# Modulation of a diffusion layer: seven of twelve weight blocks multiplied in high and low parts, two row tiles scaled by ScalarE

## Chip, cores and metric

One core of a Trainium2 chip. The metric is the device time of one execution in microseconds, median of several runs. The two last decimals are the hardware profiler's.

## What is computed

The reference is one layer of a token generator: adaLN-modulated RMSNorm, two token mixers, a merge, a mixture of experts. The change lies in its first step, the modulation of both streams (1024 latent tokens modulated by `c`, 256 context tokens by `c_ctx`), D = 1024:

```python
mod = silu(c) @ w_mod + b_mod           # 6 * 1024 columns
shift, scale = mod[..., :1024], mod[..., 1024:2048]
h = rms_norm(x, g) * (1 + scale) + shift
...
```

The further four thousand columns of `mod` are gates and the shift and scale of the second norm. All in float32; the big products of the kernel use the type fp32r, with each operand split into a high part (the value rounded to fp32r) and a low part (the rest).

## The kernel before

The program is a row of stages with a barrier between them; the first after the constants is `front` (line 173), the next `project_qk`. Each stage is written by hand as five instruction streams with semaphores: SyncE (the weights' DMA queue), ScalarE, GpSimd, TensorE, VectorE.

`front` works on twelve blocks of 512 columns of `w_mod` (`NB = 12`), 128 partitions x 8 x 512 in float32, 2 MB each, in three slots of `fr_w`. SyncE loads a block when the one three before is multiplied (L217), its bias behind it (L223). TensorE multiplies (`rows`, L312): the stationary side is `fr_c`, two columns (silu of `c` and of `c_ctx`), the moving side 512 columns of the weights, eight pieces k that add up in `fr_rows_ps`, float32, which the engine works off as sixteen records. VectorE takes the 2 x 512 result and adds the bias (`take`, L352). TensorE then turns it into columns for the first four blocks (`out`, L323, four transposes into 128 x 8), or spreads it over 128 partitions for the other eight (L326), ScalarE moves it out of PSUM (`move`, L271 and L277), and SyncE stores the spread rows (L230).

Blocks 4 to 8 carry two of the ten token tiles each (128 tokens, `tiles_before`): ScalarE normalises a tile (`normalise`: square with sum L255, L257, L260, scale L264) and asks for the next but one (L250); TensorE turns it (L334); VectorE scales and shifts it in eight pieces (`leave`, L361) and casts the high part (L366), GpSimd subtracts the low part (L302). Tiles 0 and 1 are normalised before the first `move`. At the start of the stage GpSimd makes the masks of later stages (`build_masks`, L147 to L170), among them 28 affine selects on `level_mask` (L162, L164), each waiting for the one before.

The streams around the change:

```python
            normalise(0)
            normalise(1)
            for n in range(NB):
                move(n)
                for t in tiles_before(n):
                    if t + 2 < NT:
                        normalise(t + 2)
```

```python
            for n in range(NB):      # TensorE
                rows(n)
                for t in tiles_before(n):
                    turn(t)
                out(n)
```

## Time and profile before

| | |
|---|---|
| median of 3 runs | 2454.72 us (2452.33 to 2458.88) |
| profiled execution | 2456.33 us, span 2454.6 us |
| mean granted clock of TensorE | 0.942 |
| TensorE busy | 2175.8 us, 89% of the span |
| VectorE, ScalarE, GpSimd busy | 1420.3, 1013.2, 854.0 us |
| `front`, first transfer to the first of the next stage | 6.1 to 131.7 us |

Busy shares are means over stages with different limits; the stage in question is 125 of 2454 us, 5%. A row of the order of time gives when an instruction started, how long it lasted, and in brackets how long its engine had been idle and who ended that; a row of the waits gives the sum for one waiting line. L numbers are lines of the kernel before, and lines of the changed kernel where the text says so.

### The profile page before, as it was taken

How to read it: one execution, taken by the hardware profiler on the slowest of the kernel's cores; microseconds unless marked ns; L12 is line 12 of the kernel's file. 1: busy time of each engine (PE TensorE's matmuls, PEld its weight loads, DVE VectorE, ACT ScalarE, POOL GpSimd, SP SyncE). 2: the span in 40 equal slices, each digit the busy share in tenths (PEclk: the TensorE clock that was granted, in tenths of full speed). 3: DMA queues.
4: the chain of work that ended last, by engine and by line, in shares of the span. 5: the costliest groups of instructions: out<-in, count | busy, mean ns of one | idle time of the engine just before them, and what ended most of it. 6: DMA issues, size and time to landing. Idle time of an engine off the chain costs nothing. (4 is left out here: it accounts for less than half of the span.)

```text
span 2454.6 us, 26795 instructions
## 1 busy us (share of the span) xinstructions
PE 2175.8 (89%) x10286; PEld 1757.6 (72%) x10286; DVE 1420.3 (58%) x1711; ACT 1013.2 (41%) x1266; POOL 854.0 (35%) x630
## 2 busy tenths in 40 slices
PE   6979997998798994899999779999659999999992
PEld 1268886887687883788888657788557788887882
DVE  0529642110333323888988445434258899998993
ACT  1422310111244443455555344432226666766762
POOL 5300000110356662567766422210113344443541
PEclk9989998999899996899999989999859999999996
DMA  7733226211754665243454386563359966369425
GB/s 277 252 72 101 74 56 219 82 48 47 248 172 156 184 154 184 86 129 109 128 134 121 86 263 190 174 194 117 109 214 338 366 221 198 98 196 341 146 53 163
DMA packets 263146, 398.75 MB, mean 162 GB/s; under 512 B 27302, under 2 KB 187174, under 8 KB 256236
## 3 DMA queue, kind: packets, MB, share of 16 engines
q1 hardware_dynamic: 233324, 243.90, 31.3%
q0 software_dynamic: 27968, 147.89, 19.2%
q10 hardware_dynamic: 1728, 5.25, 0.6%
q8 instruction: 83, 1.36, 0.2%
q14 instruction: 43, 0.35, 0.0%
HBM read 401.68 MB, written 88.67 MB: 200 GB/s over the span
## 5 line engine op out<-in xcount | busy, mean ns | idle before, releaser
L2600 DVE TENSOR_TENSOR ex_w_lo<-ex_raw,ex_w_hi 128x2048 fp32r<-128x2048 f32 x186 | 415.9, 2285 | 38.5 <-ACT ex_w_hi L2462 38.2
L2462 ACT ACTIVATE ex_w_hi<-ex_raw 128x2048 fp32r<-128x2048 f32 x182 | 337.8, 1909 | 170.9 <-DMA ex_raw<-in_w_up_dram,rt_w_rows 88.9
L816 POOL DMA_DIRECT2D vals<-rows_stage x40 | 21.8, 545 | 449.7 <-ACT rows_stage L808 449.7
L2332 POOL DMA_INDIRECT ex_raw<-in_w_up_dram,rt_w_rows x60 | 78.0, 1299 | 137.3 <-DVE ex_w_lo L2600 126.1
L2025 DVE TENSOR_TENSOR mo_w_lo<-mo_w,mo_w_hi 128x1024 fp32r<-128x1024 f32 x48 | 59.2, 1234 | 98.6 <-ACT mo_w_hi L1922 98.6
L1557 PEld LDWEIGHTS gl_lv_ps<-gl_q_level,gl_k_level 128*128 128x128 f32 x896 | 108.2, 194 | 11.2 <-issue 8.3
L2332 POOL DMA_INDIRECT ex_raw<-in_w_down_dram,rt_w_rows x30 | 51.9, 1730 | 183.2 <-DVE ex_w_lo L2600 176.9
L1557 PE MATMUL gl_lv_ps<-gl_q_level,gl_k_level 128*128 128x64 f32 x896 | 110.4, 276 | 3.7 <-DVE gl_scores L1687 2.0
L808 ACT ACTIVATE rows_stage<-rows_ps 128x512 f32<-128x512 f32 x40 | 23.9, 598 | 214.2 <-PE rows_ps L785 214.2
L901 PE MATMUL gl_u_ps<-half_hi,gl_u_w_hi 128*128 128x512 f32 x256 | 107.8, 421 | 4.4 <-ACT gl_u_exp L919 4.4
L901 PE MATMUL ml_u_ps<-half_hi,ml_u_w_hi 128*128 128x512 f32 x256 | 104.9, 410 | 6.5 <-ACT ml_u_exp L919 6.5
L2391 PE MATMUL ex_g_ps<-ex_w_hi,ex_x_hi 128*128 128x512 f32 x248 | 102.4, 413 | 6.5 <-DVE ex_x_lo L2605 6.5
L2391 PE MATMUL ex_y_ps<-ex_w_hi,ex_hidden_hi 128*128 128x512 f32 x248 | 100.3, 404 | 7.1 <-DVE ex_w_lo L2600 7.1
L2136 PE MATMUL mo_ps<-mo_branch_hi,mo_w_hi 128*128 128x512 f32 x256 | 104.8, 409 | 1.4 <-POOL mo_branch_lo L1990 1.0
L2137 PE MATMUL mo_ps<-mo_branch_hi,mo_w_lo 128*128 128x512 f32 x256 | 102.7, 401 | 0.0
L2138 PE MATMUL mo_ps<-mo_branch_lo,mo_w_hi 128*128 128x512 f32 x256 | 102.6, 401 | 0.0
L903 PE MATMUL gl_u_ps<-half_hi,gl_u_w_lo 128*128 128x512 f32 x256 | 101.3, 396 | 0.0
L902 PE MATMUL gl_u_ps<-half_lo,gl_u_w_hi 128*128 128x512 f32 x256 | 101.2, 395 | 0.0
L903 PE MATMUL ml_u_ps<-half_hi,ml_u_w_lo 128*128 128x512 f32 x256 | 101.1, 395 | 0.0
L902 PE MATMUL ml_u_ps<-half_lo,ml_u_w_hi 128*128 128x512 f32 x256 | 101.0, 395 | 0.0
L2392 PE MATMUL ex_g_ps<-ex_w_lo,ex_x_hi 128*128 128x512 f32 x248 | 99.0, 399 | 0.0
L2393 PE MATMUL ex_g_ps<-ex_w_hi,ex_x_lo 128*128 128x512 f32 x248 | 98.6, 398 | 0.0
(403 smaller groups left out, 6079.3 us busy)
## 6 DMA issues: line engine op xcount, KB each, us to landing
fr_w<-in_w_mod_dram SPq DMA_DIRECT2D x12, 2048.0 KB, 9.8
ml_u_w<-in_w_in_dram SPq DMA_DIRECT2D x32, 512.0 KB, 5.2
gl_u_w<-in_w_in_dram SPq DMA_DIRECT2D x32, 512.0 KB, 5.2
vals<-rows_stage POOLq DMA_DIRECT2D x40, 256.0 KB, 2.3
ml_v<-vals SPq DMA_DIRECT2D x20, 512.0 KB, 4.4
gl_v<-vals SPq DMA_DIRECT2D x20, 512.0 KB, 3.3
qk_w<-in_w_in_dram SPq DMA_DIRECT2D x16, 512.0 KB, 5.0
rows_w<-in_w_in_dram SPq DMA_DIRECT2D x8, 1024.0 KB, 6.5
```

The source lines that it names most:

```text
L901: pe.matmul(self.ps[:, :], a_hi, b_hi, start=(k == 0), stop=False)
L902: pe.matmul(self.ps[:, :], a_hi, b_lo, start=False, stop=False)
L903: last = pe.matmul(self.ps[:, :], a_lo, b_hi, start=False, stop=(k == KD - 1))
L1557: last = pe.matmul(lv_ps[at_l // 2 % 2][:, lv_cols(at_l, h)], kl[:, d, l, h * P:(h + 1) * P], ql[:, l, h * P // 2:(h + 1) * P // 2], start ...
L2136: pe.matmul(out, a_hi, b_hi_, start=(k == 0), stop=False)
L2137: pe.matmul(out, a_lo, b_hi_, start=False, stop=False)
L2138: last = pe.matmul(out, a_hi, b_lo_, start=False, stop=(k == KD - 1))
L2332: pool.indirect_dma_start(out=raw[:, q, :], out_offset=None, in_=sources[q], in_offset=bass.IndirectOffsetOnAxis(ap=w_rows[:, q, b:b + 1], ...
L2391: pe.matmul(dst, a_hi[:, ka], hi[:, q, at:at + 512], start=first, stop=False)
L2392: pe.matmul(dst, a_hi[:, ka], lo[:, q, at:at + 512], start=False, stop=False)
L2462: act.activation(hi[:, q, h], raw[:, q, h], ACT.Copy).then_inc(hi_done[q], 1)
L2600: dve.tensor_tensor(lo[:, q, at], raw[:, q, at], hi[:, q, at].bitcast(F32), ALU.subtract)\
```

## The change

Blocks 0 to 3 and 9 to 11 (`PARTED`) are no longer multiplied in float32. For each of their pieces k ScalarE makes the high part (`weight_hi`), VectorE the low part (`weight_lo`), TensorE multiplies both with a stationary side of four columns: the high parts of `silu(c)` and `silu(c_ctx)`, then their low parts (`c_parts`). High and low pieces lie in rings of three. The result has four rows, which `out` folds to two (`pairs`, `first`). Blocks 4 to 8 are multiplied as before. The last two tiles, 8 and 9, are scaled by ScalarE, out of PSUM, in eight pieces each, and VectorE only casts them. The bias has two slots of four rows, which GpSimd fills with zeros first. Square writes into `fr_xn` instead of a tile of its own, so the wait for the turn stands ahead of it.

```diff
+    PARTED = [n for n in range(NB) if n not in WITH_TOKENS]
+    RING = 3
...
+        LATER = WITH_TOKENS[-1] + 1
+        BY_ACT = (NT - 2, NT - 1)
...
             def normalise(t):
...
+                if t >= 2:
+                    act.wait_ge(turned, t - 1)
+                act.activation(xn[:, j, :], xt[:, j, :], ACT.Square, accum_out=st[:, t, 0:1]).then_inc(stat, 1)
...
+            def weight_hi(n, first, last):
+                act.wait_ge(w_loaded[n % SLOTS], 16 * (n // SLOTS) + 16)
+                for k in range(first, last):
+                    at = piece(n, k)
+                    if at >= RING:
+                        act.wait_ge(piece_done, at - RING + 1)
+                    act.activation(w_hi[:, at % RING, :], wt[:, n % SLOTS, k, :], ACT.Copy).then_inc(w_hi_done, 1)
+
+            def leave(t):
...
+                for k in range(KD):
+                    last = act.activation(ht[:, t % 2, k, :], x_ps[t % 2][:, k * P:(k + 1) * P], ACT.Identity,
+                                          bias=m.mod_col[:, k, stream:stream + 1],
+                                          scale=m.a1[:, k, stream:stream + 1])
+                last.then_inc(scaled_by_act, 1)
...
+            weight_hi(0, 0, KD)
             normalise(0)
-            normalise(1)
             for n in range(NB):
+                if n + 1 in PARTED and n + 1 != LATER:
+                    weight_hi(n + 1, 0, KD)
+                for t in tiles_before(n):
+                    if t in BY_ACT:
+                        leave(t)
                 move(n)
+                if n == 0:
+                    normalise(1)
                 for t in tiles_before(n):
                     if t + 2 < NT:
                         normalise(t + 2)
+                if n + 2 == LATER:
+                    weight_hi(LATER, 0, RING)
+                if n + 1 == LATER:
+                    weight_hi(LATER, RING, KD)
...
+            pool.memset(bias[:, :, :], 0.0).then_inc(bias_cleared, 1)
+            pool.memset(first[:, :], 0.0).then_inc(first_ready, 1)
+            pool.memset(pairs[:, :], 0.0).then_inc(first_ready, 1)
...
+            def rows_in_parts(n):
+                if n >= 2:
+                    pe.wait_ge(row_ready, n - 1)
+                for k in range(KD):
+                    at = piece(n, k)
+                    pe.wait_ge(w_lo_done, at + 1)
+                    out = rows_ps[n % 2][:, :]
+                    pe.matmul(out, c_parts[:, :, k], w_hi[:, at % RING, :], start=(k == 0), stop=False)
...
+            def weight_lo(n, first, last):
+                for k in range(first, last):
+                    at = piece(n, k)
+                    dve.wait_ge(w_hi_done, at + 1)
+                    if at >= RING:
+                        dve.wait_ge(piece_done, at - RING + 1)
+                    dve.tensor_tensor(w_lo[:, at % RING, :], wt[:, n % SLOTS, k, :],
+                                      w_hi[:, at % RING, :].bitcast(F32), ALU.subtract).then_inc(w_lo_done, 1)
...
+            weight_lo(0, 0, KD)
             for n in range(NB):
+                if n + 1 in PARTED and n + 1 != LATER:
+                    weight_lo(n + 1, 0, RING - 1)
                 take(n)
+                if n + 1 in PARTED and n + 1 != LATER:
+                    weight_lo(n + 1, RING - 1, KD)
...
                 for t in tiles_before(n):
                     leave(t)
+                if n + 2 == LATER:
+                    weight_lo(LATER, 0, RING)
+                if n + 1 == LATER:
+                    weight_lo(LATER, RING, KD)
```

The prediction writes hi(n,k) and lo(n,k) for the high and the low part of piece k of block n.

How the change moves instructions, at three places. First ScalarE at the start of the stage, from the tables' loading on, before (L255 to L264 is a normalisation, L250 its next load):

```order
L284 ACT_TABLE_LOAD
L255 ACTIVATE fr_junk,fr_stat<-fr_x 128x1024 [waits fr_x_loaded0]
L257 ACTIVATE fr_stat<-fr_stat,eps 128x1 [waits fr_stat]
L260 ACTIVATE fr_stat<-fr_stat 128x1 [waits fr_stat]
L264 ACTIVATE fr_xn<-fr_x,fr_stat 128x1024 [waits fr_stat]
L250 DMA fr_x<-in_x_dram 128x1024 [waits fr_xn_ready]
L255 ACTIVATE fr_junk,fr_stat<-fr_x 128x1024 [waits fr_x_loaded1]
```

and in the changed kernel (its L303 is a high part, its L286 to L293 a normalisation, its L318 the move to columns):

```order
L303 ACTIVATE fr_w_hi<-fr_w 128x512 [waits fr_w_loaded0]
L303 ACTIVATE fr_w_hi<-fr_w 128x512 x2
L303 ACTIVATE fr_w_hi<-fr_w 128x512 [waits fr_piece_done] x5
L286 ACTIVATE fr_xn,fr_stat<-fr_x 128x1024 [waits fr_x_loaded0]
L288 ACTIVATE fr_stat<-fr_stat,eps 128x1 [waits fr_stat]
L291 ACTIVATE fr_stat<-fr_stat 128x1 [waits fr_stat]
L293 ACTIVATE fr_xn<-fr_x,fr_stat 128x1024 [waits fr_stat]
L279 DMA fr_x<-in_x_dram 128x1024 [waits fr_xn_ready]
L303 ACTIVATE fr_w_hi<-fr_w 128x512 [waits fr_piece_done,fr_w_loaded1]
L303 ACTIVATE fr_w_hi<-fr_w 128x512 [waits fr_piece_done] x7
L318 ACTIVATE mod_col<-fr_out_ps 128x8 [waits fr_out_done]
L286 ACTIVATE fr_xn,fr_stat<-fr_x 128x1024 [waits fr_x_loaded1]
```

Eight high parts stand ahead of normalise(0), eight more behind it, and normalise(1) has moved behind the first move.

Second, VectorE at its start in the changed kernel (L433 is a low part, L442 a take); before, the takes stood here one behind the other:

```order
L433 TENSOR_TENSOR fr_w_lo<-fr_w,fr_w_hi 128x512 [waits fr_w_hi_done] x3
L433 TENSOR_TENSOR fr_w_lo<-fr_w,fr_w_hi 128x512 [waits fr_piece_done,fr_w_hi_done] x7
L442 TENSOR_TENSOR fr_row<-fr_rows_ps,fr_bias 4x512 [waits fr_bias_loaded0,fr_piece_done]
L433 TENSOR_TENSOR fr_w_lo<-fr_w,fr_w_hi 128x512 [waits fr_piece_done,fr_w_hi_done] x8
L442 TENSOR_TENSOR fr_row<-fr_rows_ps,fr_bias 4x512 [waits fr_bias_loaded1,fr_piece_done]
```

Rows that print alike are drawn together: of the seven low parts of the second row five belong to block 0 and two to block 1, so take(0) stands behind lo(1,0) and lo(1,1), and likewise further on.

Third, VectorE around take(8), before (L352 is a take, L361 and L366 scale and cast a tile):

```order
L366 CAST later_hi<-fr_h 128x8x128 [waits fr_scaled]
L361 TENSOR_SCALAR fr_h<-fr_x_ps,a,mod_col 128x128 [waits fr_split_lo,fr_turned]
L361 TENSOR_SCALAR fr_h<-fr_x_ps,a,mod_col 128x128 x7
L366 CAST later_hi<-fr_h 128x8x128 [waits fr_scaled]
L352 TENSOR_TENSOR fr_row<-fr_rows_ps,fr_bias 2x512 [waits fr_out_done,fr_bias_loaded2,fr_rows_done]
L361 TENSOR_SCALAR fr_h<-fr_x_ps,a,mod_col 128x128 [waits fr_split_lo,fr_turned]
```

and in the changed kernel (L451 and L459 are the scaling and the cast):

```order
L451 TENSOR_SCALAR fr_h<-fr_x_ps,a,mod_col 128x128 [waits fr_split_lo,fr_turned]
L451 TENSOR_SCALAR fr_h<-fr_x_ps,a,mod_col 128x128 x7
L459 CAST later_hi<-fr_h 128x8x128 [waits fr_scaled]
L433 TENSOR_TENSOR fr_w_lo<-fr_w,fr_w_hi 128x512 [waits fr_piece_done,fr_w_hi_done] x3
L442 TENSOR_TENSOR fr_row<-fr_rows_ps,fr_bias 2x512 [waits fr_out_done,fr_bias_loaded0,fr_rows_done]
L459 CAST later_hi<-fr_h 128x8x128 [waits fr_scaled_by_act,fr_split_lo,fr_turned] x2
L433 TENSOR_TENSOR fr_w_lo<-fr_w,fr_w_hi 128x512 [waits fr_piece_done,fr_w_hi_done] x7
L442 TENSOR_TENSOR fr_row<-fr_rows_ps,fr_bias 4x512 [waits fr_out_done,fr_bias_loaded1,fr_piece_done]
L433 TENSOR_TENSOR fr_w_lo<-fr_w,fr_w_hi 128x512 [waits fr_piece_done,fr_w_hi_done] x8
```

Three low parts of block 9 stand between the last tile of block 7 and take(8), five behind the casts of tiles 8 and 9, drawn together there with two of block 10.

## Rows read from the trace of the kernel before

**Rows 1.** Waits, 6 to 131 us: who waited for whom; us in total, times, longest.
```profile
DVE fr_row L352 <- PE fr_rows_ps L312: 78.8, 12, 21.5
```

**Rows 2.** Order of time, VectorE: start us, duration us, engine, line, operation, tiles, [idle before].
```profile
26.98 0.68 DVE L352 TENSOR_TENSOR fr_row<-fr_rows_ps,fr_bias 2x512 f32<-2x512 f32 x1 [21.54 <-PE fr_rows_ps L312]
35.12 0.68 DVE L352 TENSOR_TENSOR fr_row<-fr_rows_ps,fr_bias 2x512 f32<-2x512 f32 x1 [7.46 <-PE fr_rows_ps L312]
...
109.06 0.68 DVE L352 TENSOR_TENSOR fr_row<-fr_rows_ps,fr_bias 2x512 f32<-2x512 f32 x1 [2.23 <-PE fr_rows_ps L312]
...
126.76 0.68 DVE L352 TENSOR_TENSOR fr_row<-fr_rows_ps,fr_bias 2x512 f32<-2x512 f32 x1 [8.17 <-PE fr_rows_ps L312]
```

**Rows 3.** Order of time, TensorE's first and last products, its last spread, next stage's first transfer.
```profile
17.97 8.98 PE L312 MATMUL fr_rows_ps<-fr_w,fr_c 128*2 128x512 f32 x16 [12.84 <-DMA fr_w<-in_w_mod_dram]
...
119.69 7.03 PE L312 MATMUL fr_rows_ps<-fr_w,fr_c 128*2 128x512 f32 x16
...
127.49 1.12 PE L326 MATMUL fr_out_ps<-fr_row,fr_first 2*128 2x512 f32 x2 [0.77 <-DVE fr_row L352]
...
131.74 0.39 SPq L449 DMA_DIRECT2D qk_w<-in_w_in_dram  x1
```

**Rows 4.** Order of time, TensorE at 1450 us: fp32r products of 512 columns, back to back.
```profile
1450.64 0.39 PE L2137 MATMUL mo_ps<-mo_branch_hi,mo_w_lo 128*128 128x512 f32 x1
1450.87 0.39 PE L2138 MATMUL mo_ps<-mo_branch_lo,mo_w_hi 128*128 128x512 f32 x1
```

**Rows 5.** Groups by shape (busy us, mean ns of one): a high part, a low part.
```profile
L1929 ACT ACTIVATE mo_branch_hi<-mo_branch 128x512 fp32r<-128x512 f32 x32 | 20.3, 633 | 35.6 <-DVE mo_branch L2020 35.3
...
L2049 DVE TENSOR_TENSOR mo_y_lo<-mo_part,mo_y_hi 128x512 fp32r<-128x512 f32 x16 | 10.9, 684 | 0.0
```

**Rows 6.** Order of time, ScalarE: the first row of normalise(0), and of normalise(1).
```profile
14.81 1.06 ACT L255 ACTIVATE fr_junk<-fr_x 128x1024 bf16<-128x1024 f32 x1 [2.01 <-DMA fr_x<-in_ctx_dram]
...
18.11 1.06 ACT L255 ACTIVATE fr_junk<-fr_x 128x1024 bf16<-128x1024 f32 x1 [0.41 <-ACT fr_xn L264]
```

**Rows 7.** Order of time, GpSimd: selects of the masks, the last at 39.06.
```profile
7.95 1.10 POOL L152 TENSOR_SCALAR_AFFINE_SELECT row_of<-row_of 36x1024 f32<-36x1024 f32 x1
...
12.26 2.12 POOL L162 TENSOR_SCALAR_AFFINE_SELECT level_mask<-level_mask 128x256 int8<-128x256 int8 x1
...
39.06 0.46 POOL L164 TENSOR_SCALAR_AFFINE_SELECT level_mask<-level_mask 128x256 int8<-128x256 int8 x1
```

**Rows 8.** Order of time at 695 us: a GpSimd subtraction, a VectorE addition, both from SBUF.
```profile
695.72 2.42 POOL L890 TENSOR_TENSOR ml_u_w_lo<-ml_u_w,ml_u_w_hi 128x1024 fp32r<-128x1024 f32 x1 [0.20 <-ACT ml_u_w_hi L884]
...
696.80 1.89 DVE L1220 TENSOR_TENSOR ml_expo<-ml_rows,g_col 128x512 f32<-128x512 f32 x1
```

**Rows 9.** The same stretch further on, and all instances of the select (ns min/median/max).
```profile
698.61 0.68 DVE L1222 TENSOR_TENSOR ml_qi<-qm,ml_rows 128x512 f32<-128x512 f32 x1
...
698.84 0.95 POOL L1073 TENSOR_SCALAR_AFFINE_SELECT ml_expo<-ml_expo 128x512 f32<-128x512 f32 x1 [0.70 <-DVE ml_expo L1220]
...
L1073 POOL TENSOR_SCALAR_AFFINE_SELECT ml_expo<-ml_expo x16: 946/949/1088, 638.1 to 900.9; 128x512 f32<-128x512 f32 x16
```

**Rows 10.** Order of time at 1035 us: a one-input multiply on GpSimd, a multiply on VectorE.
```profile
1035.33 1.92 POOL L924 TENSOR_SCALAR gl_u_exp<-gl_u_exp 128x512 f32<-128x512 f32 x1
1036.24 0.72 DVE L1649 TENSOR_TENSOR gl_k_out<-gl_k,gl_exp 128x512 f32<-128x512 f32 x1
```

**Rows 11.** DMA issues of the page: KB each, median us from issue to landing.
```profile
fr_w<-in_w_mod_dram SPq DMA_DIRECT2D x12, 2048.0 KB, 9.8
```

**Rows 12.** Order of time before take(8): GpSimd's lo(7), ScalarE's last of normalise(9).
```profile
97.00 2.35 POOL L302 TENSOR_TENSOR later_lo<-fr_h,later_hi 128x1024 fp32r<-128x1024 f32 x1 [0.93 <-DVE later_hi L366]
97.20 1.15 ACT L264 ACTIVATE fr_xn<-fr_x,fr_stat 128x1024 f32<-128x1024 f32 x1
```

**Rows 13.** Groups by shape: ScalarE out of PSUM.
```profile
L580 ACT ACTIVATE qk_plain<-qk_ps x4: 377/378/379, 276.8 to 366.1; 128x256 f32<-128x256 f32 x4
...
L808 ACT ACTIVATE rows_stage<-rows_ps 128x512 f32<-128x512 f32 x40 | 23.9, 598 | 214.2 <-PE rows_ps L785 214.2
```

**Rows 14.** Windows: us, then busy us of PE, PEld, DVE, ACT, POOL, granted clock, DMA share, GB/s.
```profile
131.00:148.00 17.00, 5.67 (x26) 5.68 (x27) 2.36 (x2) 2.00 (x2) 3.28 (x5) 0.50 0.56 101
```

More of the change, by code:

```diff
@@ L232, in _ @@
                 load(n)
+            sp.wait_ge(bias_cleared, 1)
+            for n in range(2):
                 load_bias(n)
@@ L322, in out @@
                     for q in range(4):
-                        last = pe.transpose(out_ps[j][:, 2 * q:2 * q + 2], row[:, j, q * P:(q + 1) * P],
-                                            m.ident[0:2, 0:2])
-                else:
-                    last = pe.matmul(out_ps[j][:, :], first[:, :], row[:, j, :], start=True, stop=True)
+                        last = pe.matmul(out_ps[j][:, 2 * q:2 * q + 2], row[:, j, q * P:(q + 1) * P], pairs[:, :],
+                                         start=True, stop=True)
+                else:
+                    n_rows = parts_of(n)
+                    last = pe.matmul(out_ps[j][:, :], first[0:n_rows, :], row[0:n_rows, j, :], start=True, stop=True)
                 last.then_inc(out_done, 1)
@@ L337, in _ @@
             pe.wait_ge(c_ready, 1)
[L338 removed]
+            pe.wait_ge(c_split, 2)
+            pe.wait_ge(first_ready, 6)
             for n in range(NB):
[L340 removed]
+                if n in PARTED:
+                    rows_in_parts(n)
+                else:
+                    rows(n)
                 for t in tiles_before(n):
@@ L359, in leave @@
                     dve.wait_ge(split_lo, t - 1)
-                for k in range(KD):
+                for k in range(KD) if t not in BY_ACT else ():
                     last = dve.tensor_scalar(ht[:, t % 2, k, :], x_ps[t % 2][:, k * P:(k + 1) * P],
```

87 lines of the change are left out of this document (58 added, 29 removed).

## Prediction

> **What bounds the kernel now.** The page's own chain of waits ends in the last stage and never reaches the changed one, so the first stage is read from its waits and its order of time. The only long wait of the stage is VectorE's, for TensorE's rows, before each of the twelve takes [rows 1]; TensorE itself waited once for the weights, until 17.97 us [rows 3]. So TensorE sets the pace: the takes start at 26.98, 35.12 and so on to 126.76 [rows 2]. They lie 8.13 us apart up to the fifth, then 9.91 in the five that follow a block with token tiles ((109.06 - 26.98 - 4 x 8.13) / 5) and 8.85 in the last two. A block's sixteen products take 7.03 us, then take and spread follow [rows 3]. rows(0) took 8.98 us, since TensorE still ran at half its later speed until about 22. The next stage starts at 131.74, 4.98 us after the last take [rows 3]; what moves the last take moves the end. ScalarE, VectorE and GpSimd have slack in blocks 0 to 3: that slack is what the change spends.
>
> **A parted block, by itself.** Sixteen products of 0.43 us become sixteen of single-pass type. The nearest kind, 512 columns of fp32r, starts every 0.23 us and takes 0.39 to its end [rows 4]; four stationary columns cost the moving side nothing that a row here shows. But a piece now passes through three engines: ScalarE's high part 0.63 (a 128x512 copy to fp32r), VectorE's low part 0.69 (the nearest subtraction) [rows 5], then the pair of products, 0.23 + 0.39, and three hand-offs of at most 0.05, the gap between the last take and its spread [rows 3]: 2.07 us. With a ring of three pieces a piece comes out every 2.07/3 = 0.69 us, and VectorE alone allows no less than 0.62 to 0.69. The order of TensorE adds one restart of the ring per block: piece 3 of the next block needs piece 0 multiplied, which stands behind out(n). I take 6.4 us for a block that ends in columns (8.13 now) and 7.1 for one that ends in a spread (8.85 now), between 5.9 (no restart) and 7.9 (TensorE at half speed, where a pair takes 0.9 and the ring turns in 2.5). An undisturbed parted block thus gives back 1.7 us. Of the seven, blocks 0, 1 and 9 are disturbed, as follows.
>
> **Block 0.** Before, TensorE started the moment the weights landed. Three costs stand here.
> (1) The pipeline fills: 0.63 + 0.69 us before the first product, products end about 26.2 (26.4 now).
> (2) take(0) is queued behind lo(1,0) and lo(1,1) on VectorE. Those need hi(1,0), which ScalarE makes only after normalise(0), now behind hi(0) instead of before the weights landed: 3.3 us of ScalarE that 14.81 to 18.06 hid in the wait for DMA [rows 6]. take(0) then starts at about 29.6: +2.6.
> (3) GpSimd builds its masks from 12.26 to 39.5, 28 affine selects back to back, 0.46 to 2.12 us each [rows 7]; its own new work (fills of 4 partitions, four small selects) puts them 2.4 us later. Up to now VectorE had nothing with two SBUF inputs in this time: its takes read PSUM. Every lo does.
>
> **Do they hold each other up?** The trace has the collision elsewhere. A VectorE instruction of 0.68 us with two SBUF inputs took 1.89 when a two-input GpSimd subtraction was running, and ended 0.55 after it [rows 8]. For one-input selects the evidence is indirect: the select of 128x512 lasted 0.95 to 1.09 in all sixteen cases, a two-input VectorE instruction beside it, and ended 0.50 us behind that one [rows 9], while a select of 1024 elements a partition needs 1.10 [rows 7], so 512 need some 0.55. It waited. Against it: a one-input multiply on GpSimd (1.92 us) ran right through a VectorE instruction of two inputs that took no more than 0.72 [rows 10]. I take it that selects and lo exclude each other, because the select is the very instruction in question.
>
> The Trainium skill has a rule for this (SBUF — State Buffer, "Who interferes with whom"): a VectorE instruction with two SBUF inputs contends with any GpSimd instruction that reads SBUF, and whichever starts first keeps the shared ports to its end. By that rule, the trace agrees for the subtraction and for the select, and does not for the multiply; the sum would be the one taken here.
>
> **Block 0 with exclusion.** The first lo is ready at 18.65 and waits for the second long select, to 19.1. From there lo and select alternate: eight lo, 0.69 or, after a wait, 0.55 as in [rows 8] (5.0) and seven selects of 1.27, 1.26, 0.91, 0.89, 0.65, 0.63, 0.52 less what overlaps at their starts (6.1 less 0.9): last lo ends at 29.3. ScalarE's hi(0,7) is two pieces ahead, 27.4, then normalise(0) to 30.7, hi(1,0) to 31.3. There the second series begins with two selects of 2.12: lo(1,0) waits for one, lo(1,1) for the other, and take(0) stands behind both: 31.3 + 2.1 + 0.6 + 2.0 + 0.5 = 36.5, **+9.5** us (bounds: +2.6 without exclusion; +12 if the first lo meets a long select at its start).
>
> **Block 1.** Six lo are left after take(0), and seven selects stand between them (1.27, 1.26, 0.91, 0.89, 0.65, 0.63, 0.52). Last piece about 46. move(0) waits for out(0) and stands behind hi(1,7); then normalise(1), moved here, holds ScalarE 3.3 us before hi(2,0), at 48.0, and take(1) is behind lo(2,1): 49.3. The block takes 12.8 against 8.13, **+4.6** (bounds: +2.9 without exclusion, the 3.3 of normalise(1) alone less what a parted block gives; +6). By then the masks are done, near 48.
>
> **Blocks 2 and 3**: -0.3 (a low clock after the gaps takes most of the gain; bounds -1.7 and +0.5) and **-1.7**. **Blocks 4 to 7**: 0; TensorE has its old work, and Square into xn and the earlier wait for the turn cost nothing since xn(t) was turned a block earlier. Weights: w(3) is asked for when block 0's products end, at 30, lands some 9.8 us later [rows 11] and is needed after 57, so no wait for DMA. Bias loads need their row two blocks ahead: hidden.
>
> **Block 8.** take(8) is now behind lo(9,0..2), these behind hi(9,0..2), these behind normalise(9), which ended at 98.35, 0.8 before take(8) at 99.15 [rows 12]. Three hi and the last lo after them: 98.4 + 0.6 + 0.6 + 0.6 + 0.7, less the overlap, gives 100.9 to 101.4; lo(9,0) may also wait for GpSimd's lo(7) until 99.35 [rows 12]. **+1.8** (0.8 to 2.3).
>
> **Block 9.** The last two tiles leave through ScalarE: sixteen 128x128 from PSUM. 128x256 took 0.38 and 128x512 0.60 [rows 13]; on that line 128x128 is 0.27, total 4.3 us (6.0 if none is under 0.38). Then move(8) and hi(9,3), 5.3 after take(8) or so. The two GpSimd subtractions of 2.35 us that follow the casts fall together with lo(9,3), which waits some 2.1 us, as in [rows 8]. Five pieces remain. The block takes 11.9 against 9.91: **+2.0** (0.3 to 4).
>
> **Blocks 10 and 11**: -0.9 (ScalarE still behind) and -1.8.
>
> **Sum**: 9.5 + 4.6 - 0.3 - 1.7 + 1.8 + 2.0 - 0.9 - 1.8 = **+13.2** us. The profiled execution had 2456.33 around a span of 2454.6, so 2469.5 on its basis; the median of the runs is 1.6 lower, which gives **2468**. From the bounds of the two large terms the own range is 2463 to 2475.
>
> **Rivals.**
> A, the forecast, 0.55.
> B, **the selects don't hold VectorE** (they behave as the multiply in [rows 10]): block 0 +2.6, block 1 +3.2, then -0.1, -1.7, +1.8, +2.0, -0.9, -1.8: +5.1, 2460 (2456 to 2464). No slower than a measurement can tell: 0.3%, or 7.4 us. The mechanism is the ring itself, which feeds TensorE faster than 8.13 us a block and pays back what the displaced normalisations cost; it decides once the lo keeps its 0.69 between 19 and 48 us. 0.34, of which 0.04 land above the 0.3%.
> C, no collision at all, not with the subtractions either, contrary to [rows 8]: block 9 gives back another 2: about 2457. 0.03.
> D, **the clock**: between 131 and 148 us TensorE was busy a third of the time and was granted 0.50, the lower of its two levels, 1.2 GHz [rows 14]. In blocks 0, 1 and 9 the new TensorE idles as much. If the level stays low through 2, 3 and the token blocks, whose sixteen products would take 14 instead of 7 us, one such block costs 7: 2475 to 2490. Against: a token block keeps TensorE dense, and rows(0), begun from idle, was at full speed after 4 us. 0.05.
> E, faster: an fp32r pair with four columns and short records costs so little, and ScalarE's normalisations overlap so well, that all seven blocks give 1.7 and only block 0's fill of 2.6 is lost: -9, 2446. Everything in the order of ScalarE speaks against it: 0.03.
>
> **Chances**: faster 0.04 (E and a rest), same 0.33 (B's greater part, C), slower 0.63 (A, D, B's tail). The range takes in A whole and most of B: 2457 to 2476.
>
> **What would show it.** Takes at 36.5, 49, 57, 63.5, 71.6 and, last, near 140 us; next stage near 145. The lo of blocks 0 and 1 at a mean of 1.2 to 2 us, and 0.69 in blocks 2 and 3; the masks' end at 48 instead of 42. B is shown by lo at 0.69 and selects at their old lengths throughout. Block 9's wait is shown by lo(9,3) at over 2 us beside GpSimd's subtraction. D shows as granted clock 0.50 and products at twice their length in a token block. I am wrong about the ring if blocks 3, 10 or 11 take over 8.5 us; wrong about the order if take(0) starts right behind the products of its block.

## The result, and the profile after

| | before | changed |
|---|---|---|
| median of 7 runs | 2455.68 us (2452.33 to 2462.31) | 2475.20 us (2471.66 to 2482.56) |
| profiled execution, its span | 2456.33, 2454.6 us | 2477.07, 2475.4 us |
| ratio, 95% interval | | 1.0083 (1.0065 to 1.0100) |
| first transfer of the next stage | 131.74 us | 148.53 us |

The changed kernel is slower by 19.5 us, 0.8%. Of this the changed stage accounts for 16.8 in the two profiles. The rest is in later stages, whose code is the same: they took 2322.9 us before, 2326.9 in the changed kernel, and 2320.3 to 2329.6 in the experiments that differ only in this stage. So the experiments are read by the end of the stage. Where two kernels have the same code up to some point, their takes agree there to about 0.4 us: the changed kernel and one that differs only from block 8 on have take(1) at 45.3 and 45.5, take(4) at 72.5 and 72.1. The end of the stage is less exact than that: blocks 10 and 11 took up to 2.1 and 1.4 us longer in some kernels than in others whose last blocks are the same code. For an edit in the first four blocks, take(4) is therefore given beside the end.

The takes of the changed kernel (VectorE, order of time: start, duration, engine, line, and the first transfer of the next stage) answer to [rows 2] and [rows 3]:

```profile
32.22 0.67 DVE L442 TENSOR_TENSOR fr_row<-fr_rows_ps,fr_bias 4x512 f32<-4x512 f32 x1
...
45.34 0.67 DVE L442 TENSOR_TENSOR fr_row<-fr_rows_ps,fr_bias 4x512 f32<-4x512 f32 x1
...
54.89 0.67 DVE L442 TENSOR_TENSOR fr_row<-fr_rows_ps,fr_bias 4x512 f32<-4x512 f32 x1
...
63.68 0.68 DVE L442 TENSOR_TENSOR fr_row<-fr_rows_ps,fr_bias 4x512 f32<-4x512 f32 x1 [0.72 <-PE fr_rows_ps L380]
...
72.46 0.68 DVE L442 TENSOR_TENSOR fr_row<-fr_rows_ps,fr_bias 2x512 f32<-2x512 f32 x1 [8.10 <-PE fr_rows_ps L387]
...
102.18 0.68 DVE L442 TENSOR_TENSOR fr_row<-fr_rows_ps,fr_bias 2x512 f32<-2x512 f32 x1 [2.23 <-PE fr_rows_ps L387]
...
113.97 0.67 DVE L442 TENSOR_TENSOR fr_row<-fr_rows_ps,fr_bias 2x512 f32<-2x512 f32 x1
...
127.39 0.67 DVE L442 TENSOR_TENSOR fr_row<-fr_rows_ps,fr_bias 4x512 f32<-4x512 f32 x1
...
143.25 0.68 DVE L442 TENSOR_TENSOR fr_row<-fr_rows_ps,fr_bias 4x512 f32<-4x512 f32 x1 [0.73 <-PE fr_rows_ps L380]
...
148.53 0.39 SPq L556 DMA_DIRECT2D qk_w<-in_w_in_dram  x1
```

Against before they are 5.2, 10.2, 11.6, 12.3 and 12.9 us later for takes 0 to 4, constant through the token blocks, then 14.8, 18.3, 17.5 and 16.5. Only blocks 10 and 11 were shorter than before, 8.01 and 7.85 instead of 8.85. Block 3, which neither a normalisation nor a select disturbs, took 8.79 instead of 8.13 (7.97 and 8.00 in two kernels with the same code up to there).

The waits between 6 and 148 us (who waited for whom: us in total, times, longest) no longer have one long row as in [rows 1], but a ring of rows: TensorE waits for the low parts, VectorE for the high parts, ScalarE for TensorE's products.

```profile
PEld fr_rows_ps L379 <- DVE fr_w_lo L433: 33.2, 37, 3.8
...
ACT fr_w_hi L303 <- PE fr_rows_ps L380: 28.0, 32, 4.9
...
DVE fr_w_lo L433 <- ACT fr_w_hi L303: 24.0, 23, 4.0
...
PEld fr_out_ps L398 <- DVE fr_row L442: 13.3, 4, 5.8
```

Two kinds of row in this trace point at terms that the forecast had not priced, and a third shows the collision that it had priced. First, the move of a row into columns: eight records of the product with the folding matrix behind take(0) and behind take(3), and below them the four transposes of before.

```profile
32.95 1.86 PE L398 MATMUL fr_out_ps<-fr_pairs,fr_row 4*128 4x2 f32 x8 [5.25 <-DVE fr_row L442]
...
64.41 1.05 PE L398 MATMUL fr_out_ps<-fr_pairs,fr_row 4*128 4x2 f32 x8 [0.77 <-DVE fr_row L442]
```

```profile
27.72 0.41 PE L323 MATMUL fr_out_ps<-ident,fr_row 2*128 2x2 f32 x4 [0.77 <-DVE fr_row L352]
```

1.86 us at the lower clock and 1.05 at the full one, where the four transposes took 0.41. Everything in the ring from the next block's fourth piece on stands behind it. Second, TensorE's clock. These are windows of 7 us; the columns are length, busy us (and instructions) of PE, PEld, DVE, ACT and POOL, granted clock, DMA share, GB/s:

```profile
25.00:32.00 7.00, 2.09 (x7) 0.29 (x6) 4.17 (x5) 4.99 (x9) 6.45 (x9) 1.00 0.70 241
32.00:39.00 7.00, 5.94 (x18) 2.58 (x18) 4.73 (x6) 2.52 (x4) 6.73 (x5) 0.51 0.65 248
39.00:46.00 7.00, 2.12 (x8) 0.29 (x6) 4.57 (x7) 5.05 (x10) 6.39 (x10) 0.98 0.35 108
46.00:53.00 7.00, 6.93 (x21) 3.03 (x22) 3.39 (x7) 3.19 (x6) 0.34 (x3) 0.53 0.71 267
53.00:60.00 7.00, 5.53 (x19) 2.39 (x18) 4.14 (x7) 3.18 (x7) 0.00 (x0) 0.71 0.60 206
```

TensorE was busy 2.1 of 7 us before the low stretches, and then had work but at 0.51 and 0.53, near 1.2 GHz; a pair of products took 0.86 us there and 0.47 at full clock. Third, GpSimd's selects and the low parts. The rows are a select, the low part beside it, then all low parts of two stretches (ns min, median, max):

```profile
18.67 1.55 POOL L162 TENSOR_SCALAR_AFFINE_SELECT level_mask<-level_mask 128x256 int8<-128x256 int8 x1
...
19.01 1.49 DVE L433 TENSOR_TENSOR fr_w_lo<-fr_w,fr_w_hi 128x512 fp32r<-128x512 f32 x1
...
L433 DVE TENSOR_TENSOR fr_w_lo<-fr_w,fr_w_hi x8: 693/1133/1493, 18.4 to 26.0; 128x512 fp32r<-128x512 f32 x8
...
L433 DVE TENSOR_TENSOR fr_w_lo<-fr_w,fr_w_hi x13: 670/693/693, 49.6 to 62.3; 128x512 fp32r<-128x512 f32 x13
```

The select of 1.27 us took 1.55, and the low part ended 0.27 us behind it after 1.49, instead of 0.69: some 0.4 us of its work was done beside the select. They hold each other up, but not for the whole of an instruction.

### The profile page after: what moved, and what is told of

It is laid out like the page before. It is cut to its first block and busy times, and to the rows that moved or that the text cites. A ratio compares the mean times of both kernels' runs of the same rounds, so it can differ in the third digit from the quotient of the medians.

```text
span 2475.4 us, 27014 instructions
## 1 busy us (share of the span) xinstructions
PE 2179.3 (88%) x10302; PEld 1765.7 (71%) x10302; DVE 1466.7 (59%) x1753; ACT 1051.2 (42%) x1338; POOL 867.1 (35%) x636
## 3 DMA queue, kind: packets, MB, share of 16 engines
q10 hardware_dynamic: 1728, 5.25, 0.6%
```

## The experiments

Four theories: **P**, the order on ScalarE puts two normalisations on the path; **S**, selects and low parts exclude each other; **F**, the fold costs; **K**, the gaps lower TensorE's clock, and the work behind them pays. The ends below are the first transfer of the next stage: 131.74 before, 148.53 changed.

### The normalisations moved

```diff
-            weight_hi(0, 0, KD)
             normalise(0)
+            weight_hi(0, 0, KD)
...
-                if n == 0:
+                if n == 2:
                     normalise(1)
```

> The changed kernel with normalise(0) ahead of the high parts of block 0, and normalise(1) behind move(2) instead of move(0). Theory P (ScalarE's order puts the two normalisations, 3.3 us each, on the path of takes 0 and 1): take(0) at 28 instead of 32.2, take(1) 6 to 7 earlier than 45.3, the stage ends at 141 to 143 instead of 148.5. Rival Q (GpSimd's selects are what holds blocks 0 and 1, ScalarE only waits beside them): the low parts then meet the long selects from 29.6 on all the same, less than 2.5 us is won.

take(0) came at 29.2, take(1) at 41.8, take(3) at 59.6 and take(4) at 68.3, both 4.1 us earlier than in the changed kernel. But the stage ended at 149.6. Take(0) gained 3.0 us where theory P expected 4.2; VectorE made low parts among the selects without a pause from 21.51 to 29.26, the last two of them for block 1, and take(0) stands behind these. Take(1) gained 3.6 instead of 6 to 7, since block 1 took 12.6 us all the same: its last seven low parts met the second series of selects and took 8.4 us in a row, at the lower clock for TensorE besides. In the last blocks the gain was lost again: normalise(9) had to wait 1.4 us for its tile and the move before it 2.9 for a store (block 8 took 13.6 instead of 11.8), and blocks 10 and 11 ran in part at the lower clock, 10.07 and 9.27 instead of 8.01 and 7.85. P holds for its place, not for the end of the stage.

### The selects left out

```diff
-            step(pool.affine_select(out=v, in_=v, compare_op=ALU.is_ge, fill=0.0, base=-h * d,
...
-            step(pool.affine_select(out=v, in_=v, compare_op=ALU.is_ge, fill=0.0, base=h - 1 + h * d,
...
```

> The changed kernel without the 28 affine selects of level_mask (left out; the masks stay all ones, so a later stage computes something else in the same time). If the selects hold up the low parts by exclusion: low parts of blocks 0 and 1 at 0.69 instead of 1.1 us on average, take(0) 3 earlier, take(1) 5 earlier, stage end at 143 to 144. If the low parts only stretched beside another limit (ScalarE's normalisations, a ring that TensorE turns at half speed, 0.86 a piece): low parts at 0.69 but the stage end earlier by less than 2.5.

All low parts up to 46 us took their usual time (line 429 is the low part here):

```profile
L429 DVE TENSOR_TENSOR fr_w_lo<-fr_w,fr_w_hi x19: 670/691/694, 18.6 to 42.6; 128x512 fp32r<-128x512 f32 x19
```

So the collision is shown. Take(0) came 3.0 earlier, take(1) 3.3, take(3) 4.0 and take(4) 3.9. Take(0) now stood behind normalise(0), which let the first high part of block 1 start only at 27.33, and began as soon as the two low parts were made:

```profile
27.99 1.29 DVE L429 TENSOR_TENSOR fr_w_lo<-fr_w,fr_w_hi 128x512 fp32r<-128x512 f32 x2 [3.11 <-ACT fr_w_hi L299]
29.21 0.67 DVE L438 TENSOR_TENSOR fr_row<-fr_rows_ps,fr_bias 4x512 f32<-4x512 f32 x1
```

Block 1 still took 12.8: its time now had TensorE's lower clock and normalise(1) in it. At the end 2.0 were left (146.5); again block 10 fell to the lower clock and took 10.07.

### Tiles 8 and 9 scaled by VectorE

```diff
-        BY_ACT = (NT - 2, NT - 1)
+        BY_ACT = ()
```

> The changed kernel with tiles 8 and 9 scaled by VectorE as before. ScalarE loses sixteen instructions of 0.35, 5.7 us in all, between take(8) and the high part hi(9,3); VectorE gains sixteen of 0.33 before lo(9,3). If ScalarE was the limit there, block 9 takes 2 us less than its 13.4. If the limit is what follows the tiles (the casts, then GpSimd's two subtractions that collide with lo(9,3)), within 1 us of the changed kernel either way; that is what I expect, stage end 147.5 to 149.5.

149.3. Block 9 took 14.7 instead of 13.4: VectorE, who also makes the low parts, is the worse place. So moving the scaling back to VectorE does not shorten block 9. It does not show what the sixteen scalings cost where they are. In the changed kernel the place looks so (sixteen scalings, four low parts in one row, and GpSimd's last subtraction):

```profile
113.11 5.70 ACT L310 ACTIVATE fr_h<-fr_x_ps,mod_col,a 128x128 f32<-128x128 f32 x16 [0.26 <-PE fr_x_ps L410]
...
119.86 4.65 DVE L433 TENSOR_TENSOR fr_w_lo<-fr_w,fr_w_hi 128x512 fp32r<-128x512 f32 x4
119.90 2.86 POOL L367 TENSOR_TENSOR later_lo<-fr_h,later_hi 128x1024 fp32r<-128x1024 f32 x1 [0.63 <-DVE later_hi L459]
```

The second of the four low parts took 2.84 us beside the subtraction of 2.86: that is the collision of [rows 8].

### The fold left out

```diff
-                        last = pe.matmul(out_ps[j][:, 2 * q:2 * q + 2], row[:, j, q * P:(q + 1) * P], pairs[:, :],
-                                         start=True, stop=True)
+                        last = pe.transpose(out_ps[j][:, 2 * q:2 * q + 2], row[0:2, j, q * P:(q + 1) * P],
+                                            m.ident[0:2, 0:2])
```

> The changed kernel with out(n) of the first four blocks as before: four transposes of two rows instead of four products with the folding matrix (left out: the two rows from the low parts of silu(c) are not added). The folding products took 1.86 us (1.59 at full clock) where the transposes took 0.41, and the next block's ring restarts behind them. Theory F: each of the four blocks loses this 1.2 to 1.5, stage end 4 to 6 us earlier (143 to 144.5). Rival: the fold is hidden behind ScalarE and VectorE, who prepare the next pieces: under 1.5 us in all.

At the same place as above, 0.58 instead of 1.86 us:

```profile
32.91 0.58 PE L398 MATMUL fr_out_ps<-ident,fr_row 2*128 2x2 f32 x4 [4.66 <-DVE fr_row L442]
```

Blocks 1 to 4 took 12.33, 8.06, 6.49 and 8.14 instead of 13.12, 9.54, 8.79 and 8.78: together 5.2 us less (take(4) 5.3), and block 3, at full clock, is the 6.4 that the ring was forecast to give. Not all of the 5.2 is the fold's own length. The expectation calls 1.59 its time at full clock, but the granted clock fell to 0.50 while it ran, at 56 us; at full clock it took 1.05. By these rows the fold is 0.6 us longer than the transposes at full clock and 1.3 at the lower one, 2.6 us for four folds at full clock. The rest of the 5.2 hangs on the clock: block 3, for one, ran at 0.50 from 56 to 63 us with the fold and at 1.00 without. The end is 145.2, 3.3 earlier; 2.1 went back in block 10, which took 10.15 at the lower clock.

### Three products of two columns

```diff
-                    pe.matmul(out, c_parts[:, :, k], w_hi[:, at % RING, :], start=(k == 0), stop=False)
-                    pe.matmul(out, c_parts[:, :, k], w_lo[:, at % RING, :], start=False, stop=(k == KD - 1))
+                    pe.matmul(out, c_parts[:, 0:2, k], w_hi[:, at % RING, :], start=(k == 0), stop=False)
+                    pe.matmul(out, c_parts[:, 2:4, k], w_hi[:, at % RING, :], start=False, stop=False)
+                    pe.matmul(out, c_parts[:, 0:2, k], w_lo[:, at % RING, :], start=False, stop=(k == KD - 1))
```

> The changed kernel with three products of two stationary columns a piece (high by high, low by high, high by low) instead of two of four; two rows come out, so the four transposes of before do instead of the folding products (left out: low by low, too small to see). To be set beside the run without the fold (two products a piece, takes 12.33, 8.06, 6.49 apart, block 10 10.15). Theory K (TensorE, waiting for pieces, is granted the lower clock for stretches, where a pair takes 0.86 instead of 0.47; denser work keeps the higher one): blocks 2 and 10 at 7.3 to 8.6 although TensorE has half as much more to do, stage end below 145.2. Rival: the work itself counts: at full clock 0.23 more a piece, 1 to 2 us more for every block, stage end at 150 or later.

The four transposes of before stand in place of the fold here too, so it is compared with the run before: 150.5 against 145.2. Blocks 1 to 3 took 13.4, 10.14 and 7.28, and block 9 14.71 for 13.42. The rival's end came true. Half as much work more inside the block did not keep the clock: it fell in the gaps between the blocks as before (granted 0.5 from 32 to 39 and 46 to 53), and then there was more work at the lower clock. As an experiment on K it was badly chosen, since it fills the wrong place. It suggests that the gaps between the blocks count, not the small ones between pieces.

### Four blocks in parts

Only blocks 2, 3, 10 and 11, both normalisations at the start.

```diff
-    PARTED = [n for n in range(NB) if n not in WITH_TOKENS]
+    PARTED = [2, 3, 10, 11]
...
-            weight_hi(0, 0, KD)
             normalise(0)
+            normalise(1)
```

> The changed kernel with only blocks 2, 3, 10 and 11 in parts; blocks 0, 1 and 9 in float32 as before, both normalisations at the start as before, the fold only where a block is in parts. Tests whether a block in parts gains anything where nothing else stands in its way. Theory R (the ring at full clock gives back 1.7 less the fold of 1.2 and its like): takes 0 and 1 as before, blocks 2 and 3 near 6.5 and 7.9, block 4 0.65 later, 10 and 11 near 8: stage end 3 us before the 131.7 of before, at 128 to 130. Theory K (the clock falls in the gaps of every block in parts): blocks 2 and 10 at 9 to 10, stage end at 131.5 to 134. In device time either is within the noise of three rounds; the stage end tells.

138.4 us, ratio 1.0020 (1.0004 to 1.0036). Blocks 2, 3, 10 and 11 took 7.16, 7.76, 8.75 and 7.20, all less than before (8.13 and 8.85), together 3.1 us; block 4 behind them took 10.42 instead of 8.13. But neither theory had the largest loss: it lay in blocks 0 and 1, which are computed as before. VectorE's first take and TensorE's float32 products on either side of it:

```profile
30.20 0.68 DVE L444 TENSOR_TENSOR fr_row<-fr_rows_ps,fr_bias 2x512 f32<-2x512 f32 x1 [15.79 <-DMA fr_bias<-in_b_mod_dram]
...
31.44 0.09 PEld L385 LDWEIGHTS fr_rows_ps<-fr_w,fr_c 128*2 128x2 f32 x2
...
41.39 0.68 DVE L444 TENSOR_TENSOR fr_row<-fr_rows_ps,fr_bias 2x512 f32<-2x512 f32 x1 [7.01 <-PE fr_rows_ps L385]
```

The take waited for the bias. The change issues both bias loads behind three weight loads of 2 MB, and the first landed at 30.2 us, 2.3 after the products were done. TensorE idled, its clock fell, and the products of block 1 took 9.91 us for 7.03.

### The same with the bias early

```diff
-            for n in range(SLOTS):
-                load(n)
+            load(0)
             sp.wait_ge(bias_cleared, 1)
             for n in range(2):
                 load_bias(n)
+            for n in range(1, SLOTS):
+                load(n)
```

> The kernel with four blocks in parts (2, 3, 10, 11) and one edit: the two first bias loads are issued behind the first weight load instead of behind the third. In that kernel take(0) waited for the bias until 30.2 us (26.98 in the kernel before), TensorE idled 3 us, and its clock stood at half for the 7 us that followed (take(1) 11.2 later instead of 8.1). Theory B+K (the queue of the bias, and the clock behind the gap): take(0) at 27.0, take(1) at 35.1 to 35.5, stage end 5.5 to 6.5 earlier than its 138.4, near 132. If only the wait counts and the low clock has another cause: take(1) still 11 behind take(0), stage end 3 earlier. The end would then stand at or under the 131.7 of before only if blocks 2, 3, 10 and 11 give back what blocks 4 and 9 cost.

Take(0) at 28.1, take(1) 8.14 later, end at 133.1: 5.3 us earlier for 2.1 us of wait removed. (It was not 27.0, as expected, because the products of block 0 took 9.84 us, for 8.98 before. The bias was there.) The granted clock from 30 to 37 us, with four blocks in parts and the bias late, then early:

```profile
30.00:37.00 7.00, 6.07 (x11) 1.36 (x12) 2.78 (x3) 1.73 (x4) 6.66 (x6) 0.53 0.80 294
```

```profile
30.00:37.00 7.00, 6.23 (x16) 1.14 (x14) 2.87 (x4) 1.67 (x3) 6.66 (x6) 1.00 0.80 293
```

0.53 and 1.00, and the two kernels differ only in the order of the loads. This is the clearest run for K: the short wait cost its length and, behind it, 3.05 us of block 1, 0.6 of block 3 and 1.6 of block 4 (1.2 came back in block 2, whose low parts met more selects once it ran earlier, and 0.9 in blocks 10 and 11).

### Block 9 in float32

```diff
-    PARTED = [n for n in range(NB) if n not in WITH_TOKENS]
+    PARTED = [0, 1, 2, 3, 10, 11]
```

> The changed kernel with block 9 in float32 as before. The high parts of block 9 no longer stand behind normalise(9) and the sixteen scalings on ScalarE, and its low parts no longer meet GpSimd's subtractions: block 8 back from 11.8 to 9.9, block 9 from 13.4 to 9.9, 10 and 11 unchanged at 8: stage end 143 instead of 148.5. If the delay only moves on to block 10 (its high parts now stand behind the same instructions): 145 or later.

145.8. Block 8 came back to 9.91. Block 9 took 11.12, not 9.9: take(9) is now queued behind lo(10,0) and lo(10,1), and these meet GpSimd's last subtraction. Blocks 10 and 11 took 8.64 and 9.27, in part at the lower clock. So most of the delay moved on to the next block, as the second reading had it.

### The gaps filled with idle work

```diff
                     rows_in_parts(n)
+                    if n < 2:
+                        for _ in range(16):
+                            pe.matmul(x_ps[0][0:2, 0:P], c_act[:, :, 0], m.ident[:, :], start=True, stop=True)
```

> The changed kernel with idle work for TensorE: behind the last product of blocks 0 and 1, sixteen small products of the identity into a PSUM bank that nobody reads before the tokens (nothing left out, results unchanged). TensorE stood idle there for 5 and 4 us and was granted the lower clock for 7 us after each. Theory K (the idle gap itself brings the clock down): it stays at its higher level from 32 to 39 and from 46 to 52, the fold takes 1.6 instead of 1.86, block 2 8.0 to 8.8 instead of 9.5; block 1, where low parts and selects meet, gains less than 1; stage end 1 to 3 earlier although nothing useful was added. Rival (the clock follows something else, as the other engines' activity): clock and block 2 as they were, stage end 0 to 1 later.

The same windows as above:

```profile
25.00:32.00 7.00, 5.92 (x39) 2.92 (x38) 4.17 (x5) 4.99 (x9) 6.45 (x9) 1.00 0.73 237
32.00:39.00 7.00, 4.16 (x20) 1.69 (x20) 6.01 (x7) 3.13 (x7) 6.73 (x5) 1.00 0.69 265
39.00:46.00 7.00, 6.15 (x47) 3.84 (x46) 4.44 (x6) 4.22 (x8) 6.39 (x10) 1.00 0.46 136
46.00:53.00 7.00, 4.80 (x19) 1.10 (x18) 5.42 (x9) 4.80 (x9) 1.29 (x3) 0.99 0.69 248
53.00:60.00 7.00, 7.00 (x22) 2.78 (x21) 3.50 (x6) 3.21 (x6) 0.00 (x0) 0.52 0.83 296
```

The clock stayed up from 32 to 53 us. Block 1 took 11.93 instead of 13.12 and block 2 7.79 instead of 9.54, take(2) came at 52.0 instead of 54.9: 2.9 us won by work that computes nothing. The fold, too, is shorter at the full clock:

```profile
33.05 1.05 PE L398 MATMUL fr_out_ps<-fr_pairs,fr_row 4*128 4x2 f32 x8 [1.66 <-DVE fr_row L445]
```

Theory K is shown in the changed kernel itself: what TensorE does in these two gaps decides the clock behind them. The end was 149.5 all the same, 1.0 later than without the idle work and not 1 to 3 earlier. The clock now fell from 53 on, in the gap before block 3, where nothing was filled; block 4, sixteen float32 products, then took 10.48 instead of 8.78, so that take(4) was 1.0 earlier and no more, and block 10 took 10.07.

### All mended together

Normalise(0) first and normalise(1) behind the high parts of block 3, the selects of `level_mask` in the next stage (GpSimd is idle there), the bias early, and the fold out of four-row transposes. VectorE adds the halves and writes the columns, so ScalarE's moves of the first four blocks are gone too:

```diff
+                        r = parts_of(n)
+                        last = pe.transpose(out_ps[j][:, 4 * q:4 * q + r], row[0:r, j, q * P:(q + 1) * P],
+                                            m.ident[0:r, 0:r])
...
+                    dve.tensor_copy(halves[:, :, :], v[:, :, 2:4]).then_inc(half_ready, 1)
+                    dve.wait_ge(half_ready, PARTED.index(n) + 1)
+                    dve.tensor_tensor(to, v[:, :, 0:2], halves[:, :, :], ALU.add).then_inc(out_moved, 1)
...
             pool.memset(rank_raw[:, :, :], 0.0).then_inc(rank_cleared, 1)
+            build_level_mask(m, pool, sem("qk_level_built"))
```

> All seven blocks in parts with four things changed together: normalise(0) ahead of block 0 and normalise(1) behind block 3's high parts, the selects of level_mask moved into the next stage, the bias loads behind the first weight load, and the fold made of transposes of four rows with VectorE adding the halves. Each alone won 0 to 3 us of the 16.8 (one by one the next wait took the place). If the waits only hide one another: takes 0 to 3 at 28, 34.6, 41.2, 47.8 (6.5 apart, the clock stays up), take(4) at 56, blocks 8 to 11 as in the changed kernel, stage end at 132 to 134. If TensorE's gaps between the pieces alone are enough to lower its clock: 8 to 9 a block, stage end at 138 to 141.

Takes 0 to 4 at 26.8, 34.0, 41.1, 47.6 and 55.7; the end at 133.8, 14.8 us before the changed kernel. Takes 0 and 3 with the transposes behind them (442 of the changed kernel is line 458 here):

```profile
26.82 0.67 DVE L458 TENSOR_TENSOR fr_row<-fr_rows_ps,fr_bias 4x512 f32<-4x512 f32 x1
...
27.55 0.41 PE L414 MATMUL fr_out_ps<-ident,fr_row 4*128 4x4 f32 x4 [1.44 <-DVE fr_row L458]
...
47.58 0.68 DVE L458 TENSOR_TENSOR fr_row<-fr_rows_ps,fr_bias 4x512 f32<-4x512 f32 x1 [0.72 <-PE fr_rows_ps L395]
48.31 0.41 PE L414 MATMUL fr_out_ps<-ident,fr_row 4*128 4x4 f32 x4 [0.77 <-DVE fr_row L458]
```

The granted clock stayed at 1.0 through all four blocks, though TensorE stood idle for 1.4 us before each of the first three transposes. One at a time the normalisations, the selects and the fold moved the end by +1.1, -2.0 and -3.3, as if the waits hid one another. But much of that is blocks 8, 10 and 11, which took longer in those runs than in the changed kernel, and block 10 does so here (10.08). At take(4) the three won 4.1, 3.9 and 5.3, 13.3 us in sum, and all together, with the bias, 16.7. So they hid one another in part only. Blocks 8 to 11 took what they took, 43.3 us in all against 37.5 before.

### Five blocks in parts

On top of the last one, with both normalisations at the start:

```diff
-    PARTED = [n for n in range(NB) if n not in WITH_TOKENS]
+    PARTED = [1, 2, 3, 10, 11]
...
-        BY_ACT = (NT - 2, NT - 1)
+        BY_ACT = ()
```

> A version meant to be faster than both: blocks 1, 2, 3, 10 and 11 in parts, 0 and 9 in float32, both normalisations at the start, tiles all scaled by VectorE, the selects of level_mask in the next stage, bias early, fold by transposes and VectorE. Takes expected at 27, 33.5, 40, 46.5, 54.6, tokens as before, block 10 and 11 at 8 and 7.2: stage end at 124 to 126, 6 to 8 us before the kernel before (0.3%, just what five rounds can tell: ratio 0.997). If the clock falls in these blocks too: stage end at 130 to 133, ratio 1.000.

End at 129.65, ratio 0.9999 (0.9987 to 1.0010). Blocks 9, 10 and 11 took 11.0, 8.6 and 9.2: in the tail, parts lose. Take(9) stands behind two low parts of block 10, TensorE idles, the clock falls. The clock also fell from 34 to 38 us and block 2 took 7.97 for 7.14, though TensorE had not been idle for more than 1.44 us at a time; idle times of 1.41 to 1.44 at the same places left it at 1.0 in the version before. So the length of the gap alone does not decide it.

### The first four only

```diff
-    PARTED = [n for n in range(NB) if n not in WITH_TOKENS]
+    PARTED = [0, 1, 2, 3]
...
-        BY_ACT = (NT - 2, NT - 1)
+        BY_ACT = ()
```

on top of the version with all mended.

> The version in which all four things are mended, with only blocks 0 to 3 in parts; 9, 10 and 11 in float32 as before, all tiles scaled by VectorE. In the last two runs the tail blocks in parts took longer than before (11.0 + 8.6 + 9.2 against 9.9 + 8.9 + 8.9), the first four shorter (take(4) at 55.7 against 59.5). Theory: gain and loss are separate: takes 0 to 4 at 26.8, 34.0, 41.1, 47.6, 55.7, then as before: stage end at 127.9, 3.8 us before the kernel before; ratio 0.998 to 0.999, at the edge of what five rounds tell. If the loss in the tail came from the mending itself (tokens' loads, stores): stage end at 129 or later.

End at 127.98, as expected; blocks 4 to 11 took exactly their times of before. The next stage did not pay for the selects that it took over: the stage behind it starts its first load at 369.2, against 373.0 in the kernel before. In device time 2457.10 against 2460.36 on the same chip, ratio 0.9991 (0.9978 to 1.0003). It is the best version: its stage ends 20.6 us before that of the changed kernel (the spans are 2455.6 and 2475.4). That it beats the kernel before is shown for the stage (3.8 us, in one profile of each), not for the whole kernel, where the interval takes in 1.

## Why the prediction was right or wrong

The direction was right, and the median fell at the upper end of the range (2475.2, with 2475 as the end of the own range and 2476 of the wider one), but the size was not: the stage came out 16.8 us longer against 13.2, and the runs 19.5. Terms that were too large covered others that were missing. That take(3) came at 63.7, forecast 63.5, is luck: block 0 was 4.3 us too long in the forecast, and blocks 1 to 3 were 4.5 too short.

| block | forecast | profile | |
|---|---|---|---|
| 0 | +9.5 | +5.2 | collision right, its size too large |
| 1 | +4.6 | +5.0 | size right, of other parts |
| 2, 3 | -0.3, -1.7 | +1.4, +0.7 | fold missing, clock missing or too small |
| 4 to 7 | 0 | +0.7 | fold of block 3, then 0 |
| 8 | +1.8 | +1.9 | right |
| 9 | +2.0 | +3.5 | collision right, clock missing, 0.36 a scaling for 0.27 |
| 10, 11 | -0.9, -1.8 | -0.8, -1.0 | clock in block 11 |
| behind | 0 | +0.3 | |

**The fold.** The step "I take 6.4 us for a block that ends in columns" failed. It priced `out` as unchanged: four transposes, 0.41. The diff shows them replaced by products in float32 with a 4x128 stationary side. No row of before has such a product, so it should have been bounded; it took 1.86 us behind takes 0 and 1, 1.59 behind take(2) and 1.05, at full clock, behind take(3). Without it block 3 took 6.49, so the ring itself was priced rightly, though block 3, with its 8.79, passed the 8.5 that the forecast had named as the sign against the ring. With the low clock that went with it, the fold is the main error in blocks 1 to 4: 5.2 us, of which its own extra length at full clock would be 2.6.

**The clock.** It was rival D, at a chance of 0.05, and was counted into the forecast only as "a low clock after the gaps" in block 2. It was not one state that stays, as D had it. It came and went: in the changed kernel the granted clock was 0.50 from about 32 to 39, 46 to 53, 56 to 63 and 121 to 128 us and again in block 11, each time behind a gap between two blocks or inside block 9. TensorE had been idle for 5.25, 3.94, 1.24 and 3.30 us before the first four. The evidence was in the trace of before: [rows 14], and rows(0) itself. The step that failed is the reason against D, that a token block keeps TensorE dense; true of blocks 5 to 7, which is why D's extra 7 us a block did not come, and no help to blocks 1 to 3. Filling the first two gaps gave 2.9 us at take(2), and removing a wait of 2.1 gave 5.3 at the end.

**The exclusion.** That lo and select hold each other up was right, and the run without selects shows that the selects cause it: a mean of 1.14 us a low part in block 0, and 0.69 without them. It rested on thin evidence: the length of a 128x512 select was judged by its count of elements, while in [rows 7] selects of the same 128x256 took from 0.46 to 2.12. Two sizes were wrong. A low part ended only 0.27 to 0.4 us behind a select, not 0.55, so the eight of block 0 took from 18.40 to 27.01 and not from 18.65 to 29.3. And, since GpSimd was slowed less, the second series of long selects began at 29.57 and not 31.3: lo(1,0) lost 1.16 us to the first of them, and lo(1,1) slipped in between the two. take(0) came at 32.2, not 36.5. Of the rule in the Trainium skill (SBUF — State Buffer, "Who interferes with whom") the part on GpSimd's reads is borne out for affine selects. That one side is shut out for the whole instruction is too strong for them here; it fits the subtraction in block 9 (2.84 us for a low part of 0.69).

**ScalarE's order** was right at take(0) (29.2 with the normalisations moved, 32.2 without) and in block 8 (11.79 against 11.7 forecast). One reading was off: the products of block 0 end at 26.95 in the kernel before (17.97 + 8.98), not at 26.4. In the changed kernel they end at 27.70, for 26.2 forecast.

**Not seen at all**: the bias. "Bias loads need their row two blocks ahead: hidden" looked at the loads from the third on. The two first ones had moved behind 6 MB of weights, and in the version with four blocks in parts the first landed at 30.2 us. In the changed kernel take(0) came later, at 32.2, and stood behind a low part, so it cost nothing there. It became the bound once block 0 was multiplied as before. It is not what held take(0) at 29.2 when the normalisations were moved or the selects left out: there it began as soon as lo(1,1) was made, in the one run late through the selects, in the other through normalise(0).

**Rival B** is ruled out by the low parts, C by block 9 (2.84 us for a low part beside the subtraction), E by every block: none gave back 1.7.

## What stays open

Why block 10 took 8.0 us in some kernels and 10.1 in others whose last blocks are the same code: the low stretch that began in block 9 ended before 128 us in the changed kernel, and in the others it lasted well into block 10 (to 132 us without selects, to 135 with the gaps filled). What makes it end sooner or later was not separated, nor why a gap of 1.4 us lowered the clock in one version and not in another. The ends of the stage carry this difference of 2 us, and each rests on one profile. How much of block 9's 3.5 us is ScalarE's, the collision's or the clock's was not separated either. The 2.7 us by which the median grew more than the stage did in the two profiles lie in code that did not change; the rest of the kernel differs by more than that between single executions.

## What to carry to other kernels

Work taken off a dense TensorE and replaced by a chain through three engines must be priced with its gaps: TensorE's clock can fall behind one, and what follows then takes up to twice as long, so a wait of 2 us cost 5. When one edit brings several waits into one place, judge each mend close to where it acts: at the end of the stage three of them had won -1, 2 and 3 us, at take(4) 4, 4 and 5. Then look for what the last wait hides, such as a small load that was moved behind large ones. A change of a few records (a transpose for a product) on the path between two blocks is worth a row of its own in the sum, at both levels of the clock.

## What was not expected of the hardware

- Idle work made the kernel's blocks faster: sixteen products with no use behind blocks 0 and 1 brought take(2) forward by 2.9 us, because the granted clock stayed at 1.0 instead of 0.51 to 0.53. By take(4) 1.0 us of it was left, and the stage ended 1.0 later, since the clock fell further on.
- Float32 products of a 4x128 stationary with two moving columns are two records each: four took 1.05 us at full clock and 1.86 at the lower one, where four transposes of the same four rows took 0.41 (two rows at the lower clock: 0.58).
- A GpSimd affine select of int8 and a VectorE subtraction with two SBUF inputs lengthen each other in part: select from 1.27 to 1.55, subtraction from 0.69 to 1.49.
- At full clock two of three pieces followed the one before through the ring in 0.60 us (the third in some 0.88), less than the 0.69 of the slowest instruction: three low parts in a row took 1.90, so the records of VectorE overlap.
- A granted clock of 0.50 came behind idle times of TensorE of 5.25 us and of 1.24, and did not come behind others of 1.4.
